# First block's windowed attention: a job's transposes and value products three steps behind its scores, in place of two

## The chip, the cores and the metric

The kernel runs as one program on one core of a Trainium2 chip. The metric is the device time of one execution in microseconds (us). The core has five engines that each work through an instruction list of their own in order and wait for each other by semaphores: TensorE (PE in the profile, its weight loads PEld), VectorE (DVE), ScalarE (ACT), GpSimd (POOL) and SyncE (SP, which issues most transfers).

## The reference

Two transformer-like blocks are computed over 2048 tokens of width 1024, in float32. The first has windowed attention and a state-space branch, the second latent attention, a gated linear recurrence and a mixture of experts. The change lies in the first block's windowed attention alone: 8 query heads of 64 share 2 key/value heads; queries come in 16 blocks of 128, and a query block sees its own block of keys and one on each side (two blocks in all for the first and the last).

```python
scores = jnp.einsum('bnqhgd,bnkhd->bnhgqk', q, kw) * (HEAD_DIM ** -0.5)
scores = jnp.where(valid, scores + bias, NEG_INF)
m = jnp.maximum(scores.max(-1, keepdims=True), sk)      # sk: a "sink" per head
p = jnp.exp(scores - m)
probs = p / (p.sum(-1, keepdims=True) + jnp.exp(sk - m))
o = jnp.einsum('bnhgqk,bnkhd->bnqhgd', probs, vw)       # later times silu(z_attn)
```

## The kernel before

**Stages.** The kernel is a row of stages that every engine runs through in the same order (`te_norm`, `te_u`, ..., `te_qkv`, `te_win`, `te_br`, ...). `te_win`, `ve_win`, `ac_win` and `po_win_all` are the windowed attention on the four engines. Keys, queries and values are in SBUF before it begins. The stage after it (`te_br`) begins when the last two jobs are finished (`win_done`): only then does SP issue its first weight transfer.

**Jobs.** The stage has 32 jobs (`JOBS`). Job j is query block j // 2 and four of the eight heads: two key/value heads (`kv`) times `a` = 0, 1. `keys(j)` gives its key blocks: three, or two for jobs 0, 1, 30 and 31. What is done for a job, in order:

- Scores, in two halves a = 0, 1 (`te_win_score`, L1234): two products 128 x 384 into two of the PSUM banks 0 to 3. A half waits until DVE has read the same half of the job before (`P`, j-1, a).
- `ve_win_score` (L1249): adds the bias, writes the sum into the job's buffer `Pb[j % 4]` and takes the maximum. There are four such buffers. It waits until the transposes of job j-4, which had the buffer, are done.
- `ac_win_score` (L1260): exponential in place with the row sum; `ve_win_sink`, `ac_win_sink` (L1267, L1274): the sink's term.
- `ve_win_sum` (L165, L1279): sum and reciprocal. It stands in the next step on DVE, behind that step's first half of scores.
- `po_win` (L1287): POOL multiplies the four 128 x 384 pieces of the job by the reciprocals.
- `te_win_turn` (L148): for each key block u = 0, 1, 2 four transposes of 128 x 128 into bank 4 or 5. It waits for POOL's job j. `any_win_turn` copies the result out: the running number of the key block (`TURN[j] + u`) decides, even ones ACT (L153), odd ones DVE (L159). So a job with even number j >= 2 has its u = 0 and u = 2 copied by ACT and u = 1 by DVE, one with odd number the other way round.
- `te_win_pv` (L1319): two products of the transposed probabilities with V for each u; it waits for the copy.
- `ve_win_finish` (L1336): times silu(z), into `attnT`. The z tiles come in four transfers of SP (L1329), each used by eight jobs.

**Order.** It is written out by hand. In step j of the loop PE issues: score(j, 0), pv(j-3, 2), turn(j-2, 0), turn(j-2, 1), score(j, 1), pv(j-2, 0), turn(j-2, 2), pv(j-2, 1). DVE: score half 0 of j, sum of j-1, its copies of u = 0, 1 of j-2, score half 1 and sink of j, finish of j-3, its copy of u = 2 of j-2. ACT: exponentials of half 0 of j, its copies of u = 0, 1 of j-2, exponentials of half 1 and sink of j, its copy of u = 2. POOL takes the jobs one after the other and has nothing else to do in this stage. A wait that an earlier wait of the same engine on the same semaphore already covers is not issued (`Lane.wait_ge`).

Of the kernel before, what the change touches and what calls it, by code (L numbers as in the profile page):

```python
# [28 lines left out]
class Counts:  # L29
# [12 lines left out]
    def inc(self, name, *event, by=1):  # L42
        self.count[name] = self.count.get(name, 0) + by
        if event:
            self.value[(name,) + event] = self.count[name]
        return self.sem(name), by
# [4 lines left out]
    def at(self, name, *event):  # L51

        if any(isinstance(x, int) and x < 0 for x in event):
            return self.sem(name), 0
        return self.sem(name), self.value[(name,) + event] if self.emits else 0
# [36 lines left out]
def build(nc, T, out):  # L92
    ctx = ExitStack()
    with ctx:
# [35 lines left out]
        def bank(i, n=512):  # L130
            return pst[:, i, 0:n]
# [14 lines left out]
        def trs(t, pairs):  # L146
            for o, i in pairs:
                x = t.do.transpose(o, i, ident[0:i.shape[0], 0:i.shape[0]])  # L148
            return x

        def acopy(a, o, i, scale=None, bias=None):
            if scale is None and bias is None:
                return a.do.activation(o, i, ACT.Copy)  # L153
            return a.do.activation(o, i, ACT.Identity, bias=0.0 if bias is None else bias,  # L154
                                   scale=1.0 if scale is None else scale)

        def vcopy(v, o, i, scale=None, bias=None):
            if scale is None and bias is None:
                return v.do.tensor_copy(o, i)  # L159
            if bias is None:  # L160
                return v.do.tensor_scalar(o, i, scale, None, MUL)
            return v.do.tensor_scalar(o, i, 1.0 if scale is None else scale, bias, MUL, ADD)
# [882 lines left out]
        def qkv_evac(n):  # L1045
            return at("qkv_ve" if n % 2 else "qkv_ac", "tile", n)

        def qkv_done(e):
            e.wait_ge(*qkv_evac(22))
            e.wait_ge(*qkv_evac(23))  # L1050
# [157 lines left out]
        JOBS = 2 * NT  # L1208

        def keys(j):  # L1210
            n = j // 2
            return max(0, n - 1), min(NT, n + 2)

        TURN = [sum(keys(i)[1] - keys(i)[0] for i in range(j)) for j in range(JOBS + 1)]
# [8 lines left out]
        def PT_evac(x):  # L1223
            return at("win_ve" if x % 2 else "win_ac", "PT", x)

        def te_win_score(t, j, a):
            n = j // 2
            k0, k1 = keys(j)
            m = 2 * (j % 2) + a
            qkv_done(t)  # L1230
            t.wait_ge(*(at("win_ve", "P", j - 1, a, 1) if j else qkv_evac(23)))
            for kv in range(2):
                rows = slice(kv * 64, kv * 64 + 64)
                x = t.do.matmul(bank(2 * a + kv)[:, 0:(k1 - k0) * 128], qT[m][rows, n * 128:(n + 1) * 128],  # L1234
                                kT[rows, k0 * 128:k1 * 128], start=True, stop=True)
            x.then_inc(*inc("win_pe", "score", j, a))

        def ve_win_score(v, j, a):
            n = j // 2
            k0, k1 = keys(j)  # L1240
            nk, c0 = (k1 - k0) * 128, (k0 - n + 1) * 128
            v.wait_ge(*at("win_pe", "score", j, a))
            v.wait_ge(*at("ld_bias", "bias"))
            v.wait_ge(*at("bias_ve", "nsk"))
            v.wait_ge(*at("win_pe", "PT", TURN[j - 3] - 1) if j >= 4 else at("mod_ve", "mod"))
            for kv in range(2):
                x, h = head(j, a, kv)
                c = j % 4 * 4 + x
                v.do.tensor_tensor_reduce(Pb[j % 4][:, x, 0:nk], bank(2 * a + kv)[:, 0:nk], bias[:, h, c0:c0 + nk],  # L1249
                                          1.0, nsk[:, h:h + 1], ADD, MIN, mx[:, c:c + 1]  # L1250
                                          ).then_inc(*inc("win_ve", "P", j, a, kv))
# [38 lines left out]
        def te_win_turn(t, j, u):  # L1290
            if u >= keys(j)[1] - keys(j)[0]:
                return
            x = TURN[j] + u
            t.wait_ge(*at("win_po", "P", j))
            t.wait_ge(*(PT_evac(x - 2) if x >= 2 else qkv_evac(22 - x)))
            trs(t, [(bank(4 + x % 2)[:, i * 128:(i + 1) * 128], Pb[j % 4][:, i, u * 128:(u + 1) * 128])
                    for i in range(4)]).then_inc(*inc("win_pe", "PT", x))

        def any_win_turn(e, j, u):
            x = TURN[j] + u  # L1300
            if u >= keys(j)[1] - keys(j)[0]:
                return
            e.wait_ge(*at("win_pe", "PT", x))
            e.wait_ge(*at("win_pe", "PV", x - 4))
            if x % 2:
                vcopy(e, PT[x % 4], bank(4 + x % 2)).then_inc(*inc("win_ve", "PT", x))
            else:
                acopy(e, PT[x % 4], bank(4 + x % 2)).then_inc(*inc("win_ac", "PT", x))

        def te_win_pv(t, j, u):  # L1310
            k0, k1 = keys(j)
            if u >= k1 - k0:
                return
            x = TURN[j] + u
            t.wait_ge(*PT_evac(x))
            if u == 0:
                t.wait_ge(*(at("win_ve", "O", j - 2) if j >= 2 else (qkv_evac(23), at("mod_ve", "mod"))[j]))
            for kv in range(2):
                o = t.do.matmul(bank(6 + j % 2)[kv * 64:kv * 64 + 64, 0:256], V[:, k0 + u, kv * 64:kv * 64 + 64],  # L1319
                                PT[x % 4][:, kv * 256:kv * 256 + 256], start=(u == 0), stop=(u == k1 - k0 - 1))  # L1320
            o.then_inc(*inc("win_pe", "PV", x))
# [10 lines left out]
        def ve_win_finish(v, j):  # L1332
            n, m = j // 2, 2 * (j % 2)
            v.wait_ge(*at("win_pe", "PV", TURN[j + 1] - 1))
            v.wait_ge(*at(f"ld_z{n // 4 % 2}", "za", n // 4))
            v.do.tensor_tensor(attnT[:, m:m + 2, n * 128:(n + 1) * 128],  # L1336
                               bank(6 + j % 2)[:, 0:256].rearrange("p (a b) -> p a b", a=2),
                               Zb[n // 4 % 2][:, m:m + 2, n % 4 * 128:(n % 4 + 1) * 128], MUL
                               ).then_inc(*inc("win_ve", "O", j))

        def win_jobs(j):

            return 0 <= j < JOBS

        def te_win(t):
            for j in range(JOBS + 4):
                if win_jobs(j):
                    te_win_score(t, j, 0)
                if win_jobs(j - 3):
                    te_win_pv(t, j - 3, 2)  # L1350
                if win_jobs(j - 2):
                    te_win_turn(t, j - 2, 0)
                    te_win_turn(t, j - 2, 1)
                if win_jobs(j):
                    te_win_score(t, j, 1)
                if win_jobs(j - 2):
                    te_win_pv(t, j - 2, 0)
                    te_win_turn(t, j - 2, 2)
                    te_win_pv(t, j - 2, 1)

        def ve_win(v):
            for j in range(JOBS + 4):
                if win_jobs(j):
                    ve_win_score(v, j, 0)
                if win_jobs(j - 1):
                    ve_win_sum(v, j - 1)
                if win_jobs(j - 2):
                    for u in range(2):
                        if (TURN[j - 2] + u) % 2:
                            any_win_turn(v, j - 2, u)  # L1370
                if win_jobs(j):
                    ve_win_score(v, j, 1)
                    ve_win_sink(v, j)
                if win_jobs(j - 3):
                    ve_win_finish(v, j - 3)
                if win_jobs(j - 2) and (TURN[j - 2] + 2) % 2:
                    any_win_turn(v, j - 2, 2)

        def ac_win(a):
            for j in range(JOBS + 4):  # L1380
                if win_jobs(j):
                    ac_win_score(a, j, 0)
                if win_jobs(j - 2):
                    for u in range(2):
                        if (TURN[j - 2] + u) % 2 == 0:
                            any_win_turn(a, j - 2, u)
                if win_jobs(j):
                    ac_win_score(a, j, 1)
                    ac_win_sink(a, j)
                if win_jobs(j - 2) and (TURN[j - 2] + 2) % 2 == 0:  # L1390
                    any_win_turn(a, j - 2, 2)

        def po_win_all(p):
            for j in range(JOBS):
# [1673 lines left out]
```

## Time and profile before

| what | value |
|---|---|
| three runs | 3853.53, 3861.3, 3864.49 us; median 3861.3 us |
| the profiled execution, its own time | 3858.22 us |
| its span, first to last instruction | 3856.4 us |
| POOL's first and last multiplication of the stage (starts) | 1251.7 and 1427.3 us |
| last finish of the stage ends | 1431.26 us |
| PE, POOL, DVE, ACT busy from 1286.16 to 1410.21 us (124.05 us) | 112.69, 107.83, 90.17, 76.70 us |

Times in rows are microseconds from the start of the span. The attention stage takes some 184 us of the 3856.4. A row of a timeline is one instruction or several like it one after another: start, length, engine, line of the code, operation, what it writes and reads, how many; in brackets the engine's idle time just before and who ended it. Four transposes or four products of one score half or one key block stand as x4, and the transposes of u = 0 and u = 1 together as x8. The starts of PE's rows are measured, the ends modelled, so the pace of PE is read from start to start.

### The profile page before, as it was taken

How to read it: one execution, taken by the hardware profiler on the slowest of the kernel's cores; microseconds unless marked ns; L12 is line 12 of the kernel's file. 1: busy time of each engine (PE TensorE's matmuls, PEld its weight loads, DVE VectorE, ACT ScalarE, POOL GpSimd, SP SyncE). 2: the span in 40 equal slices, each digit the busy share in tenths (PEclk: the TensorE clock that was granted, in tenths of full speed). 3: DMA queues.
4: the chain of work that ended last, by engine and by line, in shares of the span. 5: the costliest groups of instructions: out<-in, count | busy, mean ns of one | idle time of the engine just before them, and what ended most of it. 6: DMA issues, size and time to landing. Idle time of an engine off the chain costs nothing. (4 is left out here: it accounts for less than half of the span.)

```text
span 3856.4 us, 32998 instructions
## 1 busy us (share of the span) xinstructions
PE 3514.5 (91%) x11379; PEld 1831.0 (47%) x11379; DVE 1680.2 (44%) x3966; ACT 1036.2 (27%) x2537; POOL 1015.3 (26%) x1396
## 2 busy tenths in 40 slices
PE   4999999999999889989999988999899935999997
PEld 3744455555446444434444445555555522444443
DVE  4665633343453663336665556534533340212221
ACT  3121222211100540012244446433322211222221
POOL 0377767300000870000000006645600012121211
PEclk7999999999999999999999989999989967999999
DMA  3134445433263012222310000001022205999997
GB/s 133 60 123 151 158 141 163 146 108 123 78 207 113 14 66 82 82 93 72 116 50 22 11 11 1 1 1 66 11 74 84 97 23 220 328 325 328 327 330 235
DMA packets 116746, 460.10 MB, mean 119 GB/s; under 512 B 14643, under 2 KB 42291, under 8 KB 104540
## 3 DMA queue, kind: packets, MB, share of 16 engines
q1 hardware_dynamic: 91644, 370.32, 27.0%
q0 software_dynamic: 19456, 67.15, 6.2%
q10 hardware_dynamic: 5472, 20.45, 1.4%
q8 instruction: 93, 1.52, 0.2%
q14 instruction: 81, 0.66, 0.1%
HBM read 340.35 MB, written 117.52 MB: 119 GB/s over the span
## 5 line engine op out<-in xcount | busy, mean ns | idle before, releaser
L143 PE MATMUL pst<-arena 128*128 128x512 f32 (+5 forms) x6938 | 2759.7, 556 | 88.2 <-DVE arena L159 34.1
L143 PEld LDWEIGHTS pst<-arena 128*128 128x128 f32 x6938 | 1301.9, 198 | 1424.3 <-issue 1266.5
L165 POOL TENSOR_TENSOR arena<-arena 128x4 f32<-128x4 f32 (+7 forms) x784 | 409.6, 522 | 464.2 <-DVE arena L2025 403.8
L148 PE MATMUL pst<-arena 128*128 128x128 f32 (+1 forms) x2147 | 322.4, 289 | 195.2 <-DVE arena L247 52.5
L165 DVE TENSOR_TENSOR arena<-arena 128x1 f32<-128x1 f32 (+8 forms) x1233 | 446.2, 362 | 94.5 <-ACT arena L2255 20.2
L148 PEld LDWEIGHTS pst<-arena 128*128 128x128 f32 (+1 forms) x2147 | 257.1, 147 | 353.6 <-issue 143.2
L1287 POOL TENSOR_SCALAR arena<-arena 128x384 f32<-128x384 f32 (+1 forms) x128 | 151.7, 1203 | 563.7 <-DVE arena L1279 563.7
L154 ACT ACTIVATE arena<-pst,arena 128x128 f32<-128x128 f32 (+1 forms) x630 | 244.0, 482 | 144.8 <-PE pst L148 142.3
L2202 POOL TENSOR_SCALAR arena<-arena 128x512 f32<-128x512 f32 (+3 forms) x160 | 218.8, 1386 | 172.2 <-DVE arena L165 158.6
L174 ACT ACTIVATE arena<-arena 128x1024 f32<-128x1024 f32 x48 | 50.7, 1057 | 645.5 <-DVE arena L1523 373.4
L168 DVE TENSOR_SCALAR arena<-arena 128x1 f32<-128x1 f32 (+10 forms) x569 | 139.6, 245 | 190.6 <-DMA arena<-in_bc 78.8
L2777 POOL DMA_INDIRECT out<-arena x48 | 75.8, 1579 | 494.5 <-DMA out<-arena 335.8
L171 DVE SCALAR_TENSOR_TENSOR arena<-arena,pst 128x256 f32<-128x256 f32 x96 | 43.3, 451 | 360.7 <-ACT arena L2740 359.0
L153 ACT ACTIVATE arena<-pst 128x512 f32<-128x512 f32 (+3 forms) x242 | 120.2, 517 | 253.3 <-PE pst L143 197.7
L171 DVE SCALAR_TENSOR_TENSOR arena<-arena 128x512 f32<-128x512 f32 (+4 forms) x241 | 165.3, 686 | 33.2 <-ACT arena L1736 22.1
L2249 ACT ACTIVATE arena<-pst,arena 128x512 f32<-128x512 f32 (+3 forms) x160 | 98.2, 619 | 223.5 <-DVE arena L2233 223.5
L159 DVE COPY arena<-pst 128x512 f32<-128x512 f32 (+2 forms) x202 | 108.8, 546 | 85.4 <-PE pst L148 37.7
L540 ACT ACTIVATE arena<-pst,arena 128x512 f32<-128x512 f32 x64 | 44.0, 687 | 371.8 <-PE pst L143 371.8
L2309 PE MATMUL pst<-arena 128*128 128x256 f32 (+1 forms) x576 | 141.3, 368 | 0.0
L2233 DVE TENSOR_REDUCE arena<-pst 128x2 f32<-128x1024 f32 (+2 forms) x80 | 85.2, 1065 | 126.9 <-PE pst L2217 125.8
L2740 ACT ACTIVATE arena<-pst 128x256 f32<-128x256 f32 x48 | 18.4, 384 | 452.8 <-PE pst L143 452.8
L2214 PE MATMUL pst<-arena 128*128 128x512 f32 (+3 forms) x320 | 132.5, 537 | 1.0 <-DVE arena L2035 0.9
(193 smaller groups left out, 2019.2 us busy)
## 6 DMA issues: line engine op xcount, KB each, us to landing
arena<-in_w_exp SPq DMA_DIRECT2D x48, 3072.0 KB, 12.0
arena<-in_w_ada SPq DMA_DIRECT2D x48, 512.0 KB, 4.7
rotd<-arena POOLq DMA_DIRECT2D x32, 512.0 KB, 4.0
arena<-rotd SPq DMA_DIRECT2D x32, 512.0 KB, 4.5
arena<-sgd SPq DMA_DIRECT2D x16, 1024.0 KB, 7.6
arena<-pwd SPq DMA_DIRECT2D x32, 416.0 KB, 5.6
pwd<-arena SPq DMA_DIRECT2D x16, 576.0 KB, 5.9
h2d<-arena SPq DMA_DIRECT2D x17, 512.0 KB, 2.9
```

Of the source, the lines that this page charges most:

```text
L143: x = t.do.matmul(o, l, r, start=(i == 0), stop=(i == len(pairs) - 1))
L148: x = t.do.transpose(o, i, ident[0:i.shape[0], 0:i.shape[0]])
L153: return a.do.activation(o, i, ACT.Copy)
L154: return a.do.activation(o, i, ACT.Identity, bias=0.0 if bias is None else bias, scale=1.0 if scale is None else scale)
L159: return v.do.tensor_copy(o, i)
L165: own(v, s).tensor_tensor(o, a, b, op).then_inc(*inc(s, *event))
L168: own(v, s).tensor_scalar(o, a, s1, s2, o1, o2).then_inc(*inc(s, *event))
L171: own(v, s).scalar_tensor_tensor(out=o, in0=a, scalar=sc, in1=b, op0=o1, op1=o2).then_inc(*inc(s, *event))
L1287: p.do.tensor_scalar(P_x, P_x, es[:, c:c + 1], None, MUL).then_inc(*inc("win_po", *(["P", j] if x == 3 else [])))
L2202: p.do.tensor_scalar(P_x, P_x, ff[:, r % 4, x, c:c + 1], None, MUL).then_inc(*inc("mla_po", "P", n, x))
L2214: t.do.matmul(o[x], qn[:, 2 * hp + x, tk_], kn[:, 2 * hp + x, ks], start=True, stop=False)
L2309: last_ = t.do.matmul(bank(6 + x)[:, w], V2[:, 2 * hp + x, j, :], PT2[n % 4][:, 256 * l:256 * l + 256][:, w], start=(j == 0), stop=(j == 2 ...
```

## The change

The step in which a job's transposes, copies and value products are issued is moved by one: what stood at j-2 stands at j-3, and the rest of the job (third value product, finish), which stood at j-3, stands at j-4. Scores, exponentials, sums and POOL's list stay where they are. The loops run one step longer (`JOBS + 5`). No instruction is added or removed, and the four buffers `Pb` stay four.

```diff
         def te_win(t):
-            for j in range(JOBS + 4):
+            for j in range(JOBS + 5):
                 if win_jobs(j):
                     te_win_score(t, j, 0)
+                if win_jobs(j - 4):
+                    te_win_pv(t, j - 4, 2)
                 if win_jobs(j - 3):
-                    te_win_pv(t, j - 3, 2)
-                if win_jobs(j - 2):
-                    te_win_turn(t, j - 2, 0)
-                    te_win_turn(t, j - 2, 1)
+                    te_win_turn(t, j - 3, 0)
+                    te_win_turn(t, j - 3, 1)
                 if win_jobs(j):
                     te_win_score(t, j, 1)
-                if win_jobs(j - 2):
-                    te_win_pv(t, j - 2, 0)
-                    te_win_turn(t, j - 2, 2)
-                    te_win_pv(t, j - 2, 1)
+                if win_jobs(j - 3):
+                    te_win_pv(t, j - 3, 0)
+                    te_win_turn(t, j - 3, 2)
+                    te_win_pv(t, j - 3, 1)
```

In `ve_win` the copies move from j-2 to j-3 and the finish from j-3 to j-4, in `ac_win` the copies from j-2 to j-3; `po_win_all` is as before.

## Rows read from the trace of the kernel before

**Rows 1.** The page: POOL busy tenths in 40 slices of 96.4 us.

```profile
POOL 0377767300000870000000006645600012121211
```

**Rows 2.** Waits, 1255 to 1425 us: engine, line, releaser, total us, times, longest.

```profile
POOL arena L1287 <- DVE arena L1279: 24.8, 28, 4.6
...
PE pst L148 <- POOL arena L1287: 18.7, 16, 3.3
```

**Rows 3.** Timeline of POOL in the stage.

```profile
1251.71 7.24 POOL L1287 TENSOR_SCALAR arena<-arena 128x256 f32<-128x256 f32 x8 [538.89 <-DVE arena L1279]
1263.60 9.78 POOL L1287 TENSOR_SCALAR arena<-arena 128x384 f32<-128x384 f32 x8 [4.65 <-DVE arena L1279]
...
1336.43 4.90 POOL L1287 TENSOR_SCALAR arena<-arena 128x384 f32<-128x384 f32 x4 [0.26 <-DVE arena L1279]
1342.55 4.90 POOL L1287 TENSOR_SCALAR arena<-arena 128x384 f32<-128x384 f32 x4 [1.22 <-DVE arena L1279]
```

**Rows 4.** Timeline of PE, 1336 to 1348 us: two steps.

```profile
1336.23 1.09 PE L148 MATMUL pst<-arena 128*128 128x128 f32 x8 [1.00 <-POOL arena L1287]
1337.25 0.92 PE L1234 MATMUL pst<-arena 64*128 64x384 f32 x4
1338.10 0.65 PE L1319 MATMUL pst<-arena 128*64 128x256 f32 x4
...
1339.85 0.92 PE L1234 MATMUL pst<-arena 64*128 64x384 f32 x4
1340.81 0.65 PE L1319 MATMUL pst<-arena 128*64 128x256 f32 x4
1341.39 1.09 PE L148 MATMUL pst<-arena 128*128 128x128 f32 x8
...
1345.01 0.92 PE L1234 MATMUL pst<-arena 64*128 64x384 f32 x4
1345.86 0.65 PE L1319 MATMUL pst<-arena 128*64 128x256 f32 x4
1347.50 0.77 PE L148 MATMUL pst<-arena 128*128 128x128 f32 x5 [0.99 <-POOL arena L1287]
```

**Rows 5.** Timeline of DVE in the same two steps.

```profile
1340.81 0.62 DVE L1249 CUSTOM_DVE_ANT_0 arena<-pst,arena 128x384 f32<-128x384 f32 x1 [0.90 <-PE pst L1234]
...
1342.37 0.66 DVE L159 COPY arena<-pst 128x512 f32<-128x512 f32 x1
...
1344.99 0.68 DVE L159 COPY arena<-pst 128x512 f32<-128x512 f32 x1
```

**Rows 6.** Timeline of ACT in the same two steps.

```profile
1340.18 0.57 ACT L153 ACTIVATE arena<-pst 128x512 f32<-128x512 f32 x1
...
1342.68 0.57 ACT L153 ACTIVATE arena<-pst 128x512 f32<-128x512 f32 x1
```

**Rows 7.** The sink's subtraction: duration min/median/max in ns, starts.

```profile
L1267 DVE TENSOR_TENSOR arena<-arena x32: 161/163/338, 1250.1 to 1422.7; 128x4 f32<-128x4 f32 x32
```

**Rows 8.** One stretch: us, busy by engine, granted TensorE clock, DMA, GB/s.

```profile
1255.40:1266.00 10.60, 9.91 (x48) 5.18 (x48) 5.73 (x19) 5.13 (x16) 5.95 (x6) 0.73 0.00 0
```

**Rows 9.** Timeline of all engines after the start of the stage.

```profile
1264.36 1.08 PE L1319 MATMUL pst<-arena 128*64 128x256 f32 x8 [0.68 <-ACT arena L153]
...
1265.37 0.92 PE L1234 MATMUL pst<-arena 64*128 64x384 f32 x4
...
1268.55 1.10 PE L148 MATMUL pst<-arena 128*128 128x128 f32 x8 [2.26 <-POOL arena L1287]
```

**Rows 10.** Timeline of all engines at the end of the stage.

```profile
1415.16 1.09 PE L148 MATMUL pst<-arena 128*128 128x128 f32 x8 [1.10 <-POOL arena L1287]
...
1419.20 0.65 PE L1319 MATMUL pst<-arena 128*64 128x256 f32 x4
...
1428.27 1.09 PE L148 MATMUL pst<-arena 128*128 128x128 f32 x8 [1.08 <-POOL arena L1287]
...
1430.84 0.42 DVE L1336 TENSOR_TENSOR arena<-pst,arena 128x256 f32<-128x256 f32 x1 [0.42 <-PE pst L1319]
```

More of the change, by code:

```diff
@@ L1345, in te_win @@
         def te_win(t):
-            for j in range(JOBS + 4):
+            for j in range(JOBS + 5):
                 if win_jobs(j):
                     te_win_score(t, j, 0)
+                if win_jobs(j - 4):
+                    te_win_pv(t, j - 4, 2)
                 if win_jobs(j - 3):
-                    te_win_pv(t, j - 3, 2)
-                if win_jobs(j - 2):
-                    te_win_turn(t, j - 2, 0)
-                    te_win_turn(t, j - 2, 1)
+                    te_win_turn(t, j - 3, 0)
+                    te_win_turn(t, j - 3, 1)
                 if win_jobs(j):
                     te_win_score(t, j, 1)
-                if win_jobs(j - 2):
-                    te_win_pv(t, j - 2, 0)
-                    te_win_turn(t, j - 2, 2)
-                    te_win_pv(t, j - 2, 1)
+                if win_jobs(j - 3):
+                    te_win_pv(t, j - 3, 0)
+                    te_win_turn(t, j - 3, 2)
+                    te_win_pv(t, j - 3, 1)
         def ve_win(v):
-            for j in range(JOBS + 4):
+            for j in range(JOBS + 5):
                 if win_jobs(j):
@@ L1366, in ve_win @@
                     ve_win_sum(v, j - 1)
-                if win_jobs(j - 2):
+                if win_jobs(j - 3):
                     for u in range(2):
-                        if (TURN[j - 2] + u) % 2:
-                            any_win_turn(v, j - 2, u)
+                        if (TURN[j - 3] + u) % 2:
+                            any_win_turn(v, j - 3, u)
                 if win_jobs(j):
@@ L1373, in ve_win @@
                     ve_win_sink(v, j)
[L1374 to L1377, printed above, removed]
+                if win_jobs(j - 4):
+                    ve_win_finish(v, j - 4)
+                if win_jobs(j - 3) and (TURN[j - 3] + 2) % 2:
+                    any_win_turn(v, j - 3, 2)
         def ac_win(a):
-            for j in range(JOBS + 4):
+            for j in range(JOBS + 5):
                 if win_jobs(j):
                     ac_win_score(a, j, 0)
-                if win_jobs(j - 2):
+                if win_jobs(j - 3):
                     for u in range(2):
-                        if (TURN[j - 2] + u) % 2 == 0:
-                            any_win_turn(a, j - 2, u)
+                        if (TURN[j - 3] + u) % 2 == 0:
+                            any_win_turn(a, j - 3, u)
                 if win_jobs(j):
@@ L1389, in ac_win @@
                     ac_win_sink(a, j)
-                if win_jobs(j - 2) and (TURN[j - 2] + 2) % 2 == 0:
-                    any_win_turn(a, j - 2, 2)
+                if win_jobs(j - 3) and (TURN[j - 3] + 2) % 2 == 0:
+                    any_win_turn(a, j - 3, 2)
         def po_win_all(p):
```

## Prediction, made before the changed kernel was run

> **What bounds the kernel now.** I read the page first, for where the stage lies: POOL is busy only in slices 13 and 14 around 1251 to 1431 us [rows 1], at 80 and 70%. The chain of waits is no help at this length, so the second view is the waits of that stretch: POOL and PE wait for each other, POOL 24.8 us for the reciprocals, PE 18.7 us for POOL [rows 2]. Then the timelines, engine by engine.
>
> POOL's list shows the pattern: a job takes 4.90 us, and the gaps before it alternate, 0.26 and 1.22 us [rows 3]. So two jobs take 11.28 us. The same number comes out as a loop: POOL ends a job at 1336.17 (rows 3: the one before 1336.43, less its gap of 0.26); PE starts that job's transposes at 1336.23 [rows 4], then this step's second score half, DVE, ACT; the reciprocal comes only behind the next step's first half on DVE; and POOL begins the job two further on at 1342.55. That is 6.38 us from the end of job j-2 to the start of job j, plus POOL's 4.90: 11.28 us for two jobs, 5.64 each. This loop, and not one engine's work, sets the pace: POOL needs only 4.90.
>
> The second candidate for the pace is PE. Call T the start of a step's x8 transposes. From 1336.23 to 1341.39 PE goes start to start 1.02 (second score half), 0.85 (first value product), 1.75 (transposes of u = 2, second product, on to the next first half), 0.96, 0.58: 5.16 us, and nowhere does it wait for POOL in between [rows 4]. The 0.96 is 0.85 where ACT's copy is not late (1345.01 to 1345.86), so PE's bare pace is 5.05 us. In the other step the third product starts at 1345.86, the next transposes could start 0.58 later, at 1346.44, and start at 1347.50: 1.06 us lost per two jobs [rows 4]. So even before the change only every second step waits for POOL, and what can be won per two jobs is about 1.06 us, not the 1.48 of POOL's gaps.
>
> **The change part by part.**
>
> *Waits for POOL in the steady part.* After the change the loop from POOL's end of job j-3 to its start of job j holds three jobs: (6.38 + 4.90) / 3 = 3.76 us a job, under POOL's 4.90 and PE's 5.05. POOL's job j starts 1.16 to 1.3 us after T of step j+1 (1342.55 against 1341.39), so ends by T + 6.2; its transposes come two steps later at T + 10.3. 4.1 us of slack: the wait is gone, and PE is next.
>
> *What is late next.* With PE not held, the first score half of a step starts 0.85 + 0.58 = 1.43 us before T, and DVE's pass over it 0.96 later (1339.85 to 1340.81) [rows 4, 5], at T - 0.47. ACT's copy stands behind both exponentials, 1.87 us after DVE's start (1340.81 to 1342.68) [rows 5, 6]: T + 1.40, done after 0.57, and the product follows 0.06 later (1340.18 + 0.57 against 1340.81) [rows 4, 6]: T + 2.03. PE wants it at 1.02 + 0.85 = 1.87. In steps where ACT copies u = 0 (even job) that costs 0.16, and the later copy of u = 2 then no longer holds PE: 5.21 us. Where DVE copies u = 0: start 1.56 after its pass (1342.37) [rows 5], T + 1.09, plus 0.66 and 0.06 is 1.81, before 1.87: nothing. Its copy of u = 2 starts at T + 3.60 (1344.99 - 1341.39), done 4.28, before the product at 4.47: nothing. So 5.05. A pair takes 10.26 in place of 11.28: 1.02 won. Bounds for a pair: 10.10 (ACT never late) and 11.28.
>
> *Start of the stage.* POOL's third job begins 4.65 us after the second ended (1258.95 to 1263.60) [rows 3], since its scores stood behind PE's wait for the first job. In the new order they are issued before that wait, and POOL goes on without a gap: third job done at 1258.95 + 4.90 = 1263.85. PE starts that job's transposes at 1268.55 now. Its list up to the score at 1265.37 has the same kinds and count of instructions after the first transposes, and no third product follows for a two-block job: 1265.37 + 0.85 = 1266.22 [rows 9]. Won: 2.33. In this one step DVE's pass begins at 1265.37 + 0.97 = T + 0.12 in place of T - 0.47, so ACT's copy is 0.59 later: 0.59 lost once.
>
> *The clock there.* From 1255.4 to 1266 the granted clock is 0.73 [rows 8], after PE had waited for POOL's first job: at levels of 1.2 and 2.4 GHz some 5.7 of the 10.6 us at the lower. The change puts a score half of job 2 and one of job 3 into that wait, so the clock may stay up. Worth at least 0, and at most 1266.22 - 1263.90 = 2.3 us, since POOL's third job holds the transposes till then. I take 0.9. The Trainium skill (TensorE: Matmul & The Clock Gate, section "Part 1: The HAM clock gate") says that idling lowers the clock and sustained work restores it; by that the whole 2.3 could come, but it says nothing about two score halves in such a gap.
>
> *End.* From the transposes of job 2 (1266.22) there are 12 pairs to those of job 26: 123.12 + 0.59, so 1389.93. The last steps are shorter because jobs 30 and 31 have two key blocks and then no scores are left: I put 4.99, 4.63, then 4.62 (1415.16 to 1419.20 is 4.04, plus 0.58) [rows 10], then 4.04 (no score left: four units of 0.58, and the first and last product wait for copies of 0.66 that nothing covers) and 2.5 (two key blocks). The last transposes start at 1410.7 in place of 1428.27; from there to the last finish (1430.84 + 0.42 = 1431.26) it is 2.99 us as now [rows 10]: 1413.7. These five are estimates with 1 us of doubt together. The extra step of the loop costs nothing of its own: POOL's last job ends around 1408, before its transposes are due, since its reciprocal no longer stands behind PE's wait.
>
> *Sum.* 1431.26 - 1413.7 = 17.6, plus 0.9 for the clock: 18.5. Of the 17.6, 12 x 1.02 = 12.2 come in the pairs, 2.33 - 0.59 = 1.7 at the start, the rest at the end.
>
> *Nothing elsewhere.* The next stage begins with SP's transfers after the last finish, so it moves as a whole. The z tiles' third and fourth transfer are asked for a step later than before, with nine steps of room. The buffers: DVE's scores of job j need the transposes of j-4, now in step j-1 on PE, done by T + 3.2 and needed at T + 4.6. PE issues them ahead of the scores that DVE waits for anyway, so no wait is added; if it decided, it would show as DVE waiting at L1249 beyond PE's 0.96.
>
> *A rule against it.* Sink's subtraction and the sum have both operands in SBUF. Beside a running POOL instruction the subtraction takes 163 ns in the median, 338 at most [rows 7], as POOL runs almost throughout: no sign of a hold. The Trainium skill (SBUF — State Buffer, "Who interferes with whom") says that such an instruction contends with a POOL instruction that reads SBUF, and that the one that comes second waits for the whole of the first.
>
> **The rivals.**
>
> *ACT's copy later than I think* (12%). If DVE's pass starts as late as in the first step, at T + 0.12, in every even job, 0.59 more per pair: 12 x 0.59 = 7.1 less, 11.4 us won: 3847. For it: 0.68 us of such a wait once at 1264.36 [rows 9]. Against: that step had no third product between score and transposes.
>
> *DVE and POOL hold each other* (5%). A POOL instruction is 4.90 / 4 = 1.22 us, half of it on average 0.6; laid on the sum, in front of the copy of u = 0, and on PE's next product: 0.6 in each step, 14 us over 24 steps, so 4 us won, 3854. Against it rows 7. This is what the rule named above would give.
>
> *Nothing gained* (10%). The wait for POOL covered another of nearly the same length, such as PE's on DVE for the score banks, and the pace stays 5.64: 2 us at the start, 3856.
>
> *Slower* (5%). The longer lag makes PE run ahead so that DVE's pass always falls behind T. With the pass at T + 0.12 an even step is 5.05 + 0.75 and an odd one, whose copy on DVE ends 0.12 + 1.56 + 0.66 + 0.06 = 2.40 after T, 5.05 + 0.53: 11.38 a pair, above the 11.28 of now, 1 us lost over 12 pairs, and the drain of one more job, up to 5 us, 3862 to 3864. It decides from T + 0.07 on. Against: 1.43 us of PE work between score and T, of which DVE's start takes 0.96.
>
> **How the numbers follow.** The profiled execution took 3858.2 us, of which 3856.4 are the span: 3858.2 - 18.5 = 3839.7. The median shown is 3.1 us higher, which would make 3842.8, within the range. My own case has 68%, 3836 to 3844: down to all of the clock's 2.3 and 10.10 a pair (1.4 + 1.9 + 0.6 more won), as far up for what I misread at the end and in ACT's place. I give 3840. The range of 8 in 10 reaches up to the first rival with the median's 3 us and a little more, 3852, and down to 3833, 3 us under my case. Below 0.3%, 11.6 us, a measurement of this kernel can't be told from no change. Faster by more: my case and most of the first rival, 0.82; the same: the second and third and half of the fourth, 0.15; slower: 0.03.
>
> **What would show it.** POOL's jobs without a gap from the first to about the eighth, later a gap of some 0.2 us before every job; no wait of PE for POOL after job 2; steps of PE alternating 5.2 and 5.05 us; ACT's copies as the releaser of the first product in even jobs; last finish near 1413. Wrong if PE still waits at L148 for POOL in the steady part, if a pair takes over 10.6 us, or if DVE's scores wait for transposes.

## The result, and the profile after

| | before | changed |
|---|---|---|
| median of 16 runs each | 3861.45 us | 3840.58 us |
| lowest, highest | 3847.66, 3864.78 | 3832.16, 3854.86 |
| ratio, 95% interval | | 0.995 [0.9939, 0.996] |
| profiled execution, its span | 3858.22, 3856.4 us | 3835.09, 3833.3 us |
| POOL's first start of the stage to the end of its last finish | 1251.71 to 1431.26: 179.55 us | 1245.82 to 1406.42: 160.60 us |

Faster by 0.5% (20.87 us by the medians, 15 to 24 by the interval); 3840 us was forecast. The spans differ by 23.1 us, but only 18.95 of it lie in the stage: the stage began 5.9 us earlier in this execution, and 1.7 us were lost behind it. Among the profiles below the start of the stage lies anywhere from 1234.9 to 1258.2 us, with no instruction ahead of it changed, so those 5.9 us are no effect of the change. I read everything from here on within the stage, from POOL's first start to the end of the last finish.

The waits of the stage (columns as in rows 2), 1247 to 1415 us. Against 24.8 us of POOL and 18.7 of PE [rows 2] there are 2.4 and 0.8 left; the 10.4 are gaps of the weight loads, mostly with PE at work beside them:

```profile
PEld pst L148 <- POOL arena L1287: 10.4, 24, 1.4
...
POOL arena L1287 <- DVE arena L1279: 2.4, 8, 0.3
...
PE pst L148 <- POOL arena L1287: 0.8, 1, 0.8
```

POOL's timeline, to be held against [rows 3]: its first 60 instructions run without a gap, and then it waits for each reciprocal for 0.15 or 0.32 us.

```profile
1245.82 71.02 POOL L1287 TENSOR_SCALAR arena<-arena 128x256 f32<-128x256 f32 x60 [546.30 <-DVE arena L1279]
1317.15 4.90 POOL L1287 TENSOR_SCALAR arena<-arena 128x384 f32<-128x384 f32 x4 [0.32 <-DVE arena L1279]
1322.21 4.90 POOL L1287 TENSOR_SCALAR arena<-arena 128x384 f32<-128x384 f32 x4 [0.15 <-DVE arena L1279]
```

PE's timeline in an even and an odd step, against [rows 4]. No wait for POOL is left; the even step takes 5.22 us (1331.19 to 1336.41), the odd one 5.05. The extra 0.17 lie between the second score half and the first value product: 1.01 in the even step, 0.85 in the odd.

```profile
1331.19 1.09 PE L148 MATMUL pst<-arena 128*128 128x128 f32 x8
1332.22 0.92 PE L1234 MATMUL pst<-arena 64*128 64x384 f32 x4
1333.23 0.65 PE L1319 MATMUL pst<-arena 128*64 128x256 f32 x4
...
1336.41 1.09 PE L148 MATMUL pst<-arena 128*128 128x128 f32 x8
1337.43 0.92 PE L1234 MATMUL pst<-arena 64*128 64x384 f32 x4
1338.28 0.65 PE L1319 MATMUL pst<-arena 128*64 128x256 f32 x4
...
1341.46 1.09 PE L148 MATMUL pst<-arena 128*128 128x128 f32 x8
```

DVE's first half of scores and ACT's copy of u = 0 in the same even step, against [rows 5, 6]: DVE starts at T - 0.46, the copy 1.87 later and ends at T + 1.98, the product starts at T + 2.04.

```profile
1330.73 0.62 DVE L1249 CUSTOM_DVE_ANT_0 arena<-pst,arena 128x384 f32<-128x384 f32 x1 [0.30 <-PE pst L1234]
```

```profile
1332.60 0.57 ACT L153 ACTIVATE arena<-pst 128x512 f32<-128x512 f32 x1
```

The granted clock over the 10.6 us that begin with the stage's first transposes (1249.51 here, 1255.41 before); in the same stretch of the kernel before it was 0.73 [rows 8]:

```profile
1249.50:1260.10 10.60, 9.34 (x60) 5.04 (x60) 8.45 (x33) 8.02 (x28) 10.60 (x10) 1.00 0.00 1
```

PE's transposes of jobs 2 and 3, and those of jobs 28 to 31, against [rows 9, 10]: job 2's start 12.54 us after POOL's first start, where it was 16.84.

```profile
1258.36 1.09 PE L148 MATMUL pst<-arena 128*128 128x128 f32 x8
...
1264.16 1.09 PE L148 MATMUL pst<-arena 128*128 128x128 f32 x8
```

```profile
1392.31 1.09 PE L148 MATMUL pst<-arena 128*128 128x128 f32 x8
...
1396.91 1.09 PE L148 MATMUL pst<-arena 128*128 128x128 f32 x8
...
1400.96 1.09 PE L148 MATMUL pst<-arena 128*128 128x128 f32 x8
...
1403.42 1.09 PE L148 MATMUL pst<-arena 128*128 128x128 f32 x8
```

### The profile page after: what moved, and what is told of

Read it like the earlier page. It is cut to its first block and busy times, and to the rows that moved or that the text cites. A ratio compares the mean times of both kernels' runs of the same rounds, so it can differ in the third digit from the quotient of the medians.

```text
span 3833.3 us, 32998 instructions
## 1 busy us (share of the span) xinstructions
PE 3509.7 (92%) x11379; PEld 1827.0 (48%) x11379; DVE 1678.5 (44%) x3966; ACT 1035.8 (27%) x2537; POOL 1007.0 (26%) x1396
## 5 line engine op out<-in xcount | busy, mean ns | idle before, releaser
L165 POOL TENSOR_TENSOR arena<-arena 128x4 f32<-128x4 f32 (+7 forms) x784 | 401.9, 513 | 464.3 <-DVE arena L2025 403.9
L2740 ACT ACTIVATE arena<-pst 128x256 f32<-128x256 f32 x48 | 18.5, 385 | 453.2 <-PE pst L143 453.2
```

What stands on the lines that cost most here:

```text
L165: own(v, s).tensor_tensor(o, a, b, op).then_inc(*inc(s, *event))
```

## Experiments

"Pair" is two steps in the steady part, start to start of PE's x8 transposes; "job 2" is the start of job 2's transposes from POOL's first start. An even step is the one that begins with the transposes of an even job. The changed kernel's row is the one shown above. Steps and stage come from one profile for each kernel.

| kernel | even, odd step us | job 2 | stage us |
|---|---|---|---|
| before | 5.17, 6.11 | 16.84 | 179.55 |
| changed | 5.22, 5.05 | 12.54 | 160.60 |
| e2: lag 2, half of POOL's work | 5.22, 5.05 | 11.69 | 160.09 |
| e3: lag 3, half of POOL's work | 5.22, 5.05 | 12.66 | 160.32 |
| e5: lag 2, more work on POOL | 6.14, 6.39 (12.53 a pair; 14.0 to 14.1 in the first three) | 18.29 | 204.21 |
| e6: lag 3, more work on POOL | 6.14, 6.13 | 15.36 | 194.20 |
| e1: lag 2, sum first | 5.41, 5.25 | 14.82 | 169.51 |
| e9: e1 and copy between | 5.17, 5.05 or 5.34 | 14.82 | 165.43 |
| e4: lag 3, copy between | 5.16, 5.05 | 12.20 | 159.29 |
| e10: e4 and second copy ahead | 5.07, 5.05 | 12.20 | 158.20 |
| e7: lag 2, filler on PE | 5.18, 6.10 | 14.24 | 176.93 |

**POOL's part taken out, at both lags (e2, e3).** In `po_win`, on the kernel before and on the changed one:

```diff
-            for x in range(4):
+            for x in (1, 3):
```

> The kernel before, with POOL multiplying only two of a job's four pieces (the other two stay without their reciprocal). Loop theory: the loop is (6.38 + 2.45) / 2 = 4.4 us a job, PE bounds with pairs of 10.1 to 10.3 us, stage 158 to 162 us. Rival (PE's waits are put down to POOL but come from something else of the lag of two): pairs stay at 11.3.

> The changed kernel with POOL multiplying only two of a job's four pieces. Theory (PE and the late copy of ACT bound it, POOL does not although it is busy 97%): pairs stay at 10.27 us; stage 157 to 160 us, since the first wait for POOL is shorter. Rival (POOL's work bounds the changed kernel): pairs fall towards 10.1 or less in proportion to POOL's work.

Timelines of PE with the lag of two (e2), then with three (e3):

```profile
1300.49 1.09 PE L148 MATMUL pst<-arena 128*128 128x128 f32 x8
1305.54 1.09 PE L148 MATMUL pst<-arena 128*128 128x128 f32 x8
1310.75 1.09 PE L148 MATMUL pst<-arena 128*128 128x128 f32 x8
```

```profile
1302.22 1.09 PE L148 MATMUL pst<-arena 128*128 128x128 f32 x8
1307.44 1.09 PE L148 MATMUL pst<-arena 128*128 128x128 f32 x8
1312.49 1.09 PE L148 MATMUL pst<-arena 128*128 128x128 f32 x8
```

The lag of two reaches the changed kernel's steps to 0.01 us once POOL's half of the loop is short: what the third step of lag buys is cover for POOL, nothing else, in the steady part. And the changed kernel's steps don't move when POOL's work is halved, though POOL was busy 97% of the steady part. e3's stage came out at 160.32, just above the 157 to 160 expected: I had counted a shorter first wait as won, but PE's first step then ran 5.33 us in place of 4.37. (The whole time of these two, 3914.69 and 3926.55 us, isn't compared: their values are other ones, and the mixture of experts runs more or fewer blocks by the values. Both run 11481 matmul instructions in place of 11379.)

**POOL made slower (e5, e6).** One more instruction per job in `po_win`:

```diff
+            p.do.tensor_scalar(Pb[j % 4][:, 0, 0:(k1 - k0) * 128], Pb[j % 4][:, 0, 0:(k1 - k0) * 128], 1.0, None,
+                               MUL).then_inc(*inc("win_pd", "x", j))
+            p.wait_ge(*at("win_pd", "x", j))
             for x in range(4):
```

> The kernel before (lag of two) with one more POOL instruction per job (its first piece times 1.0, waited for), some 1.3 us: POOL needs 6.2 us a job. Loop theory: (6.38 + 6.2) / 2 = 6.3 us a job, pairs of 12.5 to 12.7 us, POOL still with a gap of some 0.1 us a job; stage 197 to 201 us. Rival (a POOL-bound stage): pairs of 12.4, no gap.

> The changed kernel (lag of three) with the same one more POOL instruction per job. Loop theory: the loop over three jobs would allow (6.38 + 6.2) / 3 = 4.2 us, so POOL's own 6.2 us binds: pairs of 12.4 us, POOL without a gap from first to last, PE waiting for POOL again in every step; stage 193 to 197 us, only 3 to 5 us under the lag of two where it was 19 before. The sum and the sink's subtraction of DVE, 163 ns beside a POOL with pauses and 200 ns in the mean in the changed kernel, run longer still if a POOL without pauses holds them. Rival (the added work hides in POOL's idle time): pairs under 11.

POOL's timeline with the lag of two (e5), then with three (e6); L1284 is the added instruction:

```profile
1326.15 4.90 POOL L1290 TENSOR_SCALAR arena<-arena 128x384 f32<-128x384 f32 x4
1331.29 1.17 POOL L1284 TENSOR_SCALAR arena<-arena 128x384 f32<-128x384 f32 x1 [0.23 <-DVE arena L1279]
```

```profile
1321.60 4.90 POOL L1290 TENSOR_SCALAR arena<-arena 128x384 f32<-128x384 f32 x4
1326.47 1.17 POOL L1284 TENSOR_SCALAR arena<-arena 128x384 f32<-128x384 f32 x1
1327.74 4.90 POOL L1290 TENSOR_SCALAR arena<-arena 128x384 f32<-128x384 f32 x4
```

A job takes POOL 6.14 us (1321.60 to 1327.74). The loop at lag two then gives 6.38 + 6.14 = 12.52 us a pair; measured 12.53 from job 8 on, with a gap of 0.23 left on POOL. At lag three POOL has no gap and its own 6.14 is the pace: 12.27 a pair, a little under the 12.4 expected since the added instruction is 1.24 and not 1.3 us. In the steady part the lag is now worth 0.26 us a pair, where it was worth 1.01.

The stage of e5 came out at 204.21 us, beyond the 197 to 201 expected, and the lag is worth 10.0 us of the stage and not the 3 to 5 expected. Of this 5.4 us lie in six steps, from job 2's to job 8's transposes: 42.20 us in e5, 36.82 in e6. The pairs there take 14.09, 14.12 and 13.99 us. PE comes out of its waits for POOL (3.52, 2.37 and 2.33 us) at the lower clock. The second of these waits, and the granted clock (the figure before the last two) over the three pairs:

```profile
1284.33 1.86 PE L148 MATMUL pst<-arena 128*128 128x128 f32 x8 [2.37 <-POOL arena L1290]
1286.12 1.65 PE L1234 MATMUL pst<-arena 64*128 64x384 f32 x4
```

```profile
1270.24:1306.00 35.76, 31.01 (x168) 15.49 (x168) 20.13 (x67) 17.27 (x52) 30.21 (x25) 0.86 0.00 1
```

The transposes and the score half behind them take 3.37 us (1284.33 to 1287.70) in place of 1.87, and they are a part of the loop: 1.50 us more in the second of the three pairs, 1.45 in the third, where the pairs are 1.59 and 1.46 longer than 12.53. In the first they take 1.08 more and the pair 1.56; that rest isn't explained. From 1306 on the clock is 1.00, though PE's next wait is 2.25 us; why it stayed up from there is open. In e6 the clock is 1.00 from 1254 to 1320 us. So the loop's 6.38 us is a figure of the full clock, and a wait in the loop can make the loop itself longer.

**The loop shortened in another place (e1).** In `ve_win`, on the kernel before:

```diff
+                if win_jobs(j - 1):
+                    ve_win_sum(v, j - 1)
                 if win_jobs(j):
                     ve_win_score(v, j, 0)
-                if win_jobs(j - 1):
-                    ve_win_sum(v, j - 1)
```

> The kernel before (lag of two steps), but DVE takes the sum and reciprocal of job j-1 ahead of the first score half of job j, not behind it. Stage means from POOL's first start to the end of the last finish: 179.55 us before, 160.60 after the change. Loop theory (the wait is a loop of POOL, PE, DVE and back over two jobs): the reciprocal comes some 1.8 us earlier, the loop shrinks to (4.6 + 4.9) / 2 = 4.75 us a job, under PE's 5.05, and the lag of two is enough: pairs of 10.2 to 10.3 us, stage 162 to 165 us, the whole some 15 us faster than before. Rival (only a third job in flight helps, whatever DVE's order): pairs of 11.3 us, stage 179 us, the same time as before.

Median 3849.36 us of 10 runs, ratio to before 0.9979 [0.9961, 0.9996], and a stage of 169.51 us: about half of the gain (10.04 of 18.95 us), and neither the 15 us nor the 162 to 165 expected. Timeline of PE:

```profile
1313.62 1.09 PE L148 MATMUL pst<-arena 128*128 128x128 f32 x8
1314.64 0.92 PE L1234 MATMUL pst<-arena 64*128 64x384 f32 x4
1315.85 0.65 PE L1319 MATMUL pst<-arena 128*64 128x256 f32 x4 [0.29 <-ACT arena L153]
...
1322.65 0.92 PE L1234 MATMUL pst<-arena 64*128 64x384 f32 x4
1323.69 0.65 PE L1319 MATMUL pst<-arena 128*64 128x256 f32 x4
1324.27 1.10 PE L148 MATMUL pst<-arena 128*128 128x128 f32 x8
```

PE no longer waits for POOL in the steady part here either, so the loop was broken; but pairs are 10.66 and not 10.2 to 10.3. The wait turned into others: the sum pushes DVE's first half back from T - 0.46 to T - 0.24 in even steps, with it ACT's exponentials and the copy behind them, and the first product comes at T + 2.23. And in odd steps the third product comes 1.04 after the score, not 0.85: DVE's sink subtraction, ahead of the copy that this product waits for, takes 0.48 to 0.50 us in place of 0.16 in all twelve odd steps from job 5's on (last section). My expectation had left both out.

**What was left in e1 (e9).** e1 with ACT's copies of u = 0, 1 between the two exponentials of the first half (the edit of e4, at lag two):

> The kernel before (lag of two) with DVE's sum ahead of the first score half, as in the experiment that gave pairs of 10.66 us and a stage of 169.5, and with ACT's copy of u = 0 or 1 between the two exponentials. If what was left there against the changed kernel is the copies, late because the sum pushes DVE's first half back: even steps fall from 5.41 to about 5.16 us, odd ones stay at 5.24 or fall to 5.05, pairs 10.2 to 10.4, stage 165 to 167 us. If it is POOL's loop over two jobs after all: pairs stay at 10.66 and PE waits for POOL.

Even steps 5.17 as expected, so the copy was it; pairs 10.36 in the mean, stage 165.43. Odd steps are 5.05 and 5.34 by turns. In the long ones the sink's subtraction, which stands on DVE ahead of the copy of u = 2, takes 0.59 us in place of 0.16:

```profile
1328.89 0.59 DVE L1267 TENSOR_TENSOR arena<-arena 128x4 f32<-128x4 f32 x1
```

More on it in the last section. The rest against the changed kernel lies at the two ends: job 2's transposes 2.3 us later (the granted clock over the 10.6 us from the first transposes on is 0.77 in e9, 1.00 in the changed kernel), and 2.1 us more from those of job 28 to the end.

**The changed kernel's even steps (e4, e10).** In `ac_win`, on the changed kernel, e4 (`ac_win_score` takes the `kv` to do as a third argument):

```diff
                 if win_jobs(j):
-                    ac_win_score(a, j, 0)
+                    ac_win_score(a, j, 0, (0,))      # exponential of kv = 0
 ...
                             any_win_turn(a, j - 3, u)
                 if win_jobs(j):
+                    ac_win_score(a, j, 0, (1,))      # of kv = 1
                     ac_win_score(a, j, 1)
```

> The changed kernel, but ACT makes its copy of u = 0 or 1 between the two exponentials of the first score half, not behind both. Theory (in even jobs ACT's copy holds the first value product 0.17 us): even steps fall from 5.22 to 5.05 us, pairs from 10.27 to 10.10, stage 158 to 159 us. Rival (PE's own pace differs between the steps, or DVE's copy is as late): pairs stay at 10.27. Second rival: the exponentials come late and a new wait makes pairs longer.

Even steps fell to 5.16 only, and the stage to 159.29. PE's timeline, an even step and the start of the next:

```profile
1339.67 1.09 PE L148 MATMUL pst<-arena 128*128 128x128 f32 x8
1340.69 0.92 PE L1234 MATMUL pst<-arena 64*128 64x384 f32 x4
1341.54 0.65 PE L1319 MATMUL pst<-arena 128*64 128x256 f32 x4
...
1343.29 0.92 PE L1234 MATMUL pst<-arena 64*128 64x384 f32 x4
1344.26 0.65 PE L1319 MATMUL pst<-arena 128*64 128x256 f32 x4
1344.84 1.09 PE L148 MATMUL pst<-arena 128*128 128x128 f32 x8
```

The first product is now in time (0.85 after the score), and the third is late by 0.12 (0.97): with the first no longer in front, the copy of u = 2 holds, as in [rows 4]. The rows had said so and I forgot it. e10 moves that copy ahead of the sink's exponential as well:

```diff
                     ac_win_score(a, j, 1)
-                    ac_win_sink(a, j)
                 if win_jobs(j - 3) and (TURN[j - 3] + 2) % 2 == 0:
                     any_win_turn(a, j - 3, 2)
+                if win_jobs(j):
+                    ac_win_sink(a, j)
```

> The changed kernel with both of ACT's copies moved ahead: that of u = 0 or 1 between the exponentials of the first half (took even steps from 5.22 to 5.16), and that of u = 2 ahead of the sink's exponential (0.19 us). If the rest of 0.11 in even steps is the copy of u = 2: even steps 5.05 to 5.07, pairs 10.11, stage 157 to 158.5 us, 2 to 3 us under the changed kernel's 160.6; the whole 0.05 to 0.08% faster than it, which may not be told from no change. Rival: 5.16 stays, the copy of u = 2 is not what holds.

Even steps 5.07, PE's bare pace but for 0.02; stage 158.20. Its median is 3836.75 us of 6 runs, ratio to before 0.9931 [0.9911, 0.9952]. That interval overlaps the changed kernel's, so only the stage's own 2.4 us, from one profile each, speak for it.

**The clock at the start (e7).** In `te_win`, on the kernel before:

```diff
+                if j == 2:
+                    for _ in range(3):
+                        t.do.matmul(bank(6), kT[:, 0:128], kT[:, 0:512], start=True, stop=True)
                 if win_jobs(j - 2):
                     te_win_turn(t, j - 2, 0)
```

> The kernel before with three extra products of 128 x 512 on PE, results unused, in its wait for POOL's first job. If the low clock (0.73) after that wait comes from the wait and costs what the changed kernel won there beyond my count: clock 1.00 from 1255 us on, transposes of job 2 some 2 us nearer to POOL's first start (14.9 in place of 16.84), steady pairs unchanged at 11.28, stage 177 to 178 us. Rival (the clock falls for another reason): clock as before, 16.8 and 179.5.

```profile
1253.00:1263.60 10.60, 7.65 (x49) 3.94 (x49) 7.32 (x25) 6.49 (x20) 8.56 (x9) 1.00 0.00 1
```

PE's idle time before the first transposes (these start at 1253.01) fell from 3.32 to 0.55 us. The clock stayed at 1.00 and job 2's transposes came 2.60 us sooner, the stage 2.62 us shorter, with nothing else changed in the steady part. Both numbers are a little beyond what I expected.

## Why the prediction was right

- *Loop of 6.38 + 4.90 us over two jobs, and PE's 5.05 next.* Shown by e2, e3, e5 and e6, which move POOL's term alone. e5's pairs land within 0.01 us of the formula once the clock is full (12.53 against 12.52); where the loop would be shorter than PE's pace, in e2 and e3, pairs are the changed kernel's 10.27. The formula holds for one clock: at the lower one e5's loop was 1.5 us longer. In the changed kernel PE doesn't wait for POOL in the steady part.
- *Steps of 5.21 and 5.05.* Measured 5.22 and 5.05. ACT's copy as the cause of the longer one is shown by e4: with the copy early the first product is in time.
- *Start: 2.33 us, 0.59 lost again, clock 0 to 2.3.* Job 2's transposes came 4.30 us nearer to POOL's first start, 1.07 more than 2.33 + 0.9. If the order gave its 2.33, the clock gave 1.97, within the bound of 2.3; but that split is reckoned, not shown. By e7 the clock alone, at lag two, gives 2.60, which leaves 1.70 for the order at the full clock. No run has the new order at the clock of before. The step after it took 5.80 us, the 5.21 + 0.59 of the text.
- *Last steps 4.99, 4.63, 4.62, 4.04, 2.5, 2.99.* Measured 5.17, 4.62, 4.60, 4.05, 2.46, 3.00.
- *Sum.* 18.5 us forecast, 18.95 measured in the stage: 4.30 up to job 2's transposes, 11.17 from there to job 26's (11.65 forecast), 3.48 behind. The start gave 1.07 more than I had taken. From job 2's to job 28's transposes it took 133.95 us where my steps add to 133.33: 0.6 lost, 0.38 of it in two steps, 5.40 for 5.22 and 5.25 for 5.05, where POOL held DVE (last section), and 0.18 in the 5.17 for 4.99. That the median lies 0.6 us from 3840 is in part luck: my working led to 3842.8, and the medians differ by 20.87 us, 1.9 more than the stage explains.
- *DVE and POOL hold each other: set aside on [rows 7].* As a rival of 14 us it was rightly small, but the reading was too plain: holds exist. Most rows of before missed them by chance of timing.
- *A gap of some 0.2 us before every job of POOL from about the eighth on.* The gaps came, 0.15 and 0.32 in turn, but only from the sixteenth job on (1317 us; 60 instructions are 15 jobs). PE was earlier against POOL than I had it (job 2's transposes 12.54 us after POOL's first start, not 14.51), so the reciprocals were ready further ahead.
- *Chances.* The 0.82 for faster is added up wrongly: 0.68 and most of 0.12 make at most 0.80.

## What to carry to other kernels

When two engines wait for each other in turn, write the wait as a loop: the time from the end of one engine's job to its start of the next job that depends on it, plus the job, over the number of jobs in flight. More lag pays down to the next engine's own pace, and in steady steps it pays little once the waited-for engine is that pace itself (0.26 us a pair in e5 and e6, against 1.01). Look at the granted clock in each wait too: a wait that lowers TensorE's clock lengthens the loop of which TensorE is a part (14.1 us a pair for 12.53 in e5). Look where the loop passes through an in-order queue: moving an instruction forward there breaks the same loop, but pushes back what stood in front, and a lag costs only buffers and one more step.

## What the runs showed of the hardware

A tensor_tensor of DVE with both operands in SBUF (here 128 x 4, 0.16 us) is held by a POOL multiplication that reads SBUF, most surely when it begins in the first 0.35 us of it. The timeline of DVE in the changed kernel, while POOL ran without a gap:

```profile
1270.01 0.72 DVE L165 TENSOR_TENSOR arena<-arena 128x4 f32<-128x4 f32 x1
1272.62 0.55 DVE L1267 TENSOR_TENSOR arena<-arena 128x4 f32<-128x4 f32 x1
1275.23 0.38 DVE L165 TENSOR_TENSOR arena<-arena 128x4 f32<-128x4 f32 x1
1277.79 0.26 DVE L1267 TENSOR_TENSOR arena<-arena 128x4 f32<-128x4 f32 x1
1280.46 0.16 DVE L165 TENSOR_TENSOR arena<-arena 128x4 f32<-128x4 f32 x1
```

The lengths shrink as the start slides along POOL's instructions, one every 1.22 us: begun 0.04, 0.21 and 0.34 us after the start of one, they end 0.59 or 0.60 after it; begun at 0.57 it is not held. Of the eight of the changed kernel that begin up to 0.35 us into a POOL instruction seven are held. Later in it most are not, but some are, up to 0.6 us into the next (the 0.72), and others at the same place are not; what tells these apart is open. In e1 the eighth POOL instruction of a group begins at 1313.56 + 7 x 1.225 = 1322.13, the sink's subtraction at 1322.21 and takes 0.48:

```profile
1313.56 9.80 POOL L1287 TENSOR_SCALAR arena<-arena 128x384 f32<-128x384 f32 x8 [0.86 <-DVE arena L1279]
```

```profile
1322.21 0.48 DVE L1267 TENSOR_TENSOR arena<-arena 128x4 f32<-128x4 f32 x1
1322.96 0.67 DVE L159 COPY arena<-pst 128x512 f32<-128x512 f32 x1
```

What it costs is seen in e9, 5.34 against 5.05 us for an odd step with and without a hold of 0.43, and in the changed kernel's step of 5.25, where the sum takes 0.42 and the copy behind it lets the first product start 1.04 after the score. In e3, where POOL works half as much, the sum takes 163 ns in the mean, in the changed kernel 200, and e3's same two steps are 5.22 and 5.05 where the changed kernel had 5.40 and 5.25. How busy POOL is does not set it: in e6, where POOL has no gap at all, the sum takes 171 ns in the mean, against what I had expected: steps and POOL's instructions stand in a fixed phase, the sum 1.01 us and the sink's subtraction 0.78 us into an instruction of POOL in every steady step. The Trainium skill (SBUF — State Buffer, "Who interferes with whom") has this contention of a DVE instruction with two SBUF inputs. That the second waits for the whole of the first it says of DVE's modes with two ports; the prediction laid that at this case too, and here the clear cases waited for the first 0.6 of 1.24 us only.
